# Decay rows of the state-space branch: from matmuls to DMA, with the order of the work around them rewritten

## The chip, the cores and the metric

The kernel runs on one core of a Trainium2 chip. The metric is the device time in microseconds (us) of one execution. Three executions of the kernel before took 2516.0, 2516.44 and 2516.64 us; the median is 2516.44 us.

## The reference, cut to what matters

Two blocks of two layers each work on 512 positions of 1024 features. The change touches the first block, once in each of its two layers:

```python
h = rmsnorm(x, attn_norm_g[layer])
proj = h @ w_in[layer]
gm_u, gm_v, ssm_z, ssm_xbc, ssm_dt, da_q, da_k, da_v, gates = split_cols(proj, IN_SIZES)
y_a = chunked_spatial_gating(gelu(gm_u), gelu(gm_v), ...)
y_b = mamba2_mixer(ssm_z, ssm_xbc, ssm_dt, ...)
...
merged = g[:, :, 0] * (y_a @ w_branch_a[layer]) + g[:, :, 1] * (y_b @ w_branch_b[layer]) + ...
```

Inside `mamba2_mixer` lies the scan over four chunks of 128 positions, for 16 heads of 64 features:

```python
a_cum = jnp.cumsum(dtc * a, axis=2)
decay = exp(where(causal, a_cum[t] - a_cum[s], -inf))
y_diag = einsum('bctsgh,bcsghp->bctghp', cb[..., None] * decay, xdt)
states = einsum('bcsgn,bcsgh,bcsghp->bcghpn', bc, decay_end, xdt)
y_off  = einsum('bctgn,bcghpn,bctgh->bctghp', cc, prev, exp(a_cum))
y = y_diag + y_off + d_skip * x
```

For each head the row `a_cum` over all 512 positions is wanted on all 128 partitions: `decay` has position t along the row and position s along the partitions, and `exp(a_cum)` scales the columns of `cc`.

## The kernel before, in words

**Matmuls.** Each product with a weight is made of three float32r matmuls over 512 columns (`mm3`, L571 to L573): high part by high part, low by high, high by low. Weights come in slabs. A slab of 8 tiles of 128x128 (512 KB) is 24 matmuls; a slab of `w_branch_a` has 4 tiles (256 KB, 12 matmuls).

**A slab's way.** SyncE (SP) issues its load (`load`, L545) once the slab four places earlier has been used, since `w_raw` has four places. ScalarE (ACT) makes the high part (`hi_ahead`, L561), VectorE (DVE) the low part (`lo_ahead`, L566), both three slabs ahead of TensorE (PE). All engines work through fixed programs, each in its own order, with semaphores between them; all DMAs that load weights are issued by SP on one queue.

**Order of PE in a layer of block 1:** the slabs `gv`, `xbc` (12), `z` (8), `gu` (4), `gate_a` (8), `a` (8), `qkv` (12) and on. A bank of the accumulator `pg` holds one result; ACT or DVE must empty it before the fourth next. The small matmuls of the branches use the four banks of `pm`, numbered by the schedule `PM`.

**Scan.** `ac_keep` holds `a_cum` as 16 rows (heads) by 512. DVE splits it into two float32r parts in `ac_parts` (L1499, L1500). `ac_rows(p)` multiplies them by a column of `head_row` that stands in 128 columns, once for each head of pair p: 16 heads, 16 matmuls of 512 columns a layer (L2244), each of which puts one row on all partitions of a `pm` bank. From that bank, for each head: DVE takes the minimum with the head's column into `seg` (L1535, `bounded`), ACT makes `c_dec`, the exponential of chunks 1 to 3 (L1019), and the exponentials of the four chunks of `seg` (L1021); POOL multiplies `c_dec` by C (L2074) and the odd head's `seg` by `cb` (L2077), DVE the even head's (L1574). `seg` and `c_dec` have four places, two pairs. `y_pair(p)` (L2269, L2272) is the 14 small matmuls of a pair; DVE adds its result to `yf` (L1570).

**Where these stand.** The states of chunks 0 to 2 (L2252) are made after `gate_a` slabs 2, 4 and 6, from products that POOL makes (L2067). `ac_rows(0)` follows the last of them. In the `a` slabs PE goes: `ac_rows(p)`, slab p, `y_pair(p-1)`; the last pair falls into `qkv`. DVE in the same loop: minimum of pair p, low part of a slab, `m_val` times the slab's result (L1566), the addition (L1570), the product of the even head.

Of the kernel before, what the change touches and what calls it, by code (L numbers as in the profile page):

```python
# [7 lines left out]
F32 = mybir.dt.float32  # L8
# [105 lines left out]
def program(nc, t, out, depth=DEPTH, depth2=DEPTH):  # L114
    with ExitStack() as ctx:
# [53 lines left out]
        head_row = sb("head_row", [P, SSM_H], F32R)  # L169
# [80 lines left out]
        wt_gm = conv_in[:, 0, 4:4 + SEQ].rearrange("p (g n) -> p g n", g=GM_G)  # L250
# [6 lines left out]
        xw = [conv_in[:, 2 + g, 4:4 + SSM_I // SSM_G] for g in range(SSM_G)]  # L257
# [8 lines left out]
        ac_parts = over("ac_parts", arena_at + 4 * 26624, [P, SEQ], F32R)  # L266
# [51 lines left out]
        for name, slabs, units in [("gv", 4, 4), ("dt", 0, 1), ("xbc", 12, 12), ("z", 8, 8), ("gu", 4, 4), ("gate_a", 8, 8), ("a", 8, 8), ("qkv", 12, 12),  # L318
                                   ("gate_b", 8, 8), ("b", 8, 8), ("gate_c", 8, 8), ("c", 8, 8), ("out", 8, 8), ("up", 44, 44), ("down", 24, 8)]:
            SL.take(name, slabs)  # L320
            UN.take(name, units)
        for name, n in [("sums1", 1), ("spread1", 1), ("dt_n", 1), ("xs_n0", 2), ("ac_last", 1), ("xs_n", 6), ("gm_wt", 1), ("b_n", 2), ("cb", 2), ("gm_mix", 4)]:
            PM.take(name, n)
# [3 lines left out]
        for p in range(PAIRS + 1):  # L327
            if p < PAIRS:
                PM.take(("ac_row", p), 2)
            if p >= 1:  # L330
                PM.take(("y", p - 1), 1)
# [157 lines left out]
        def gate_unit(i):  # L489
# [10 lines left out]
                "gm_vn": TT, "decay_in": 1, "decays": 1, "dt_ready": TT, "ac_split": 1, "gm_wt_ready": 1, "ya_ready": GM_G, "ya_hi_done": GM_G,  # L500
                "ya_split": GM_G, "ac_zeroed": 1, "cb_masked": SSM_G, "seg_bound": SSM_H, "seg_exp": SSM_H, "y_init": KD, "c_exp": SSM_H, "c_scaled": SSM_H, "decay_cb_even": PAIRS, "decay_cb_odd": PAIRS, "y_sq": KD, "y_sq_added": KD - 1, "xw_ready": SSM_G * (TT - 1), "y_gated": KD, "y_rms": 1, "y_inv": 1,
                "yb_ready": KD, "yb_hi_done": 8, "yb_split": 8, "qk_ssq": TT, "qk_rms": 1, "qk_ready": 1, "lam_dot": 1, "lam_exp": 1,
                "neg_max": 2 * DA_H * TT, "w_ready": DA_H * TT, "sub_summed": 1, "sub_rms": 1, "yt_ready": DA_H, "gates_b": 1, "gate_a_last": 1, "b_merged": KD, "gates_c": 1,
# [362 lines left out]
        def _(act):  # L866
# [24 lines left out]
            act.wait_ge(setup, 8)  # L891
# [22 lines left out]
            for l in range(depth):  # L914
# [81 lines left out]
                for g in range(GM_G):  # L996
                    bank = unit_filled(act, SL["gu"] + g, UN["gu"] + g)
                    nc.scalar.activation(ya[:, g, :], bank, ACT.Gelu_apprx_tanh).then_inc(bank_free[(UN["gu"] + g) % BANKS], 1)
# [1760 lines left out]
```

## Time and profile before

| | |
|---|---|
| median of three executions | 2516.44 us |
| span of the profiled execution | 2514.7 us |
| PE busy | 2505.0 us |
| DVE, ACT, POOL busy | 1605.5, 1186.3, 317.8 us |
| granted clock of TensorE | 1.00 in every stretch asked for between 100 and 300 us |

The profiled execution's own total is not given apart from its span; its span is 1.7 us below the median of the three. A busy share says how much of the span an engine worked; a chain of waits says who stopped whom. Matmuls overlap, so the distance between the starts of two matmuls is what one costs, not its duration.

### The profile page before, as it was taken

The numbers are of one execution on the slowest core, as the hardware profiler recorded it, in microseconds if no ns is written. First come the engines' busy times: TensorE is split into PE (matmuls) and PEld (weight loads), VectorE is DVE, ScalarE is ACT, GpSimd is POOL, SyncE is SP. The second block draws the span as 40 slices with busy tenths as digits, with TensorE's granted clock in tenths as the row PEclk, the third lists the DMA queues.
The fourth block names the chain that finished last, engine by engine and source line by source line (L and its number), as shares of the span: only waits on it lengthen the run. The fifth ranks groups of instructions, "written<-read, shape, count | busy, mean of one in ns | idle before, by whom it ended". The sixth has DMA issues, their size and how long they took to land.

```text
span 2514.7 us, 34027 instructions
## 1 busy us (share of the span) xinstructions
PE 2505.0 (100%) x12261; PEld 2048.5 (81%) x12261; DVE 1605.5 (64%) x2461; ACT 1186.3 (47%) x2185; POOL 317.8 (13%) x248
## 2 busy tenths in 40 slices
PE   9999999999999999999999999999999999999999
PEld 7887887888888887887877888888888777887777
DVE  6735767567777347538767567774355777647765
ACT  6534545544333235436354443333246555564563
POOL 1024201010111000225020101110020001210010
PEclk9999999999999999999999999999999999999999
DMA  6433342333333353452444333333324322332322
GB/s 143 95 83 66 87 92 75 65 112 93 100 92 98 97 112 88 88 80 71 92 81 69 96 92 100 92 99 96 99 79 108 86 62 62 91 93 76 84 59 76
DMA packets 400031, 221.94 MB, mean 88 GB/s; under 512 B 52736, under 2 KB 377376, under 8 KB 399648
## 3 DMA queue, kind: packets, MB, share of 16 engines
q1 hardware_dynamic: 399904, 220.26, 35.7%
q8 instruction: 79, 1.29, 0.2%
q14 instruction: 48, 0.39, 0.1%
HBM read 218.12 MB, written 2.10 MB: 88 GB/s over the span
## 4 chain that ended last, share of the span: by engine, by line
PE 96%; DVE 2%; ACT 1%; issue 1%; DMA 1%; SPq 0%; DVEq 0%
PE pg L571 29%; PE pg L572 28%; PE pg L573 28%; PE pm L671 3%; PE pm L2465 1%; PE pm L2349 1%; PE pm L2439 1%; PE pm L2314 1%; PE pm L2269 1%; DVE w_lo L566 1%; PE pm L2479 1%; PE pm L2506 1%; ACT w_hi L561 0%; PE pm L2272 0%; PE pm L2252 0%
## 5 line engine op out<-in xcount | busy, mean ns | idle before, releaser
L566 DVE TENSOR_TENSOR w_lo<-w_raw,w_hi 128x1024 fp32r<-128x1024 f32 (+3 forms) x440 | 538.8, 1226 | 516.3 <-ACT w_hi L561 514.4
L571 PE MATMUL pg<-h_hi,w_hi 128*128 128x512 f32 x1856 | 737.1, 397 | 0.3 <-ACT arena L1229 0.2
L573 PE MATMUL pg<-h_hi,w_lo 128*128 128x512 f32 x1856 | 723.3, 390 | 0.0
L572 PE MATMUL pg<-h_lo,w_hi 128*128 128x512 f32 x1856 | 723.1, 390 | 0.0
L561 ACT ACTIVATE w_hi<-w_raw 128x1024 fp32r<-128x1024 f32 (+3 forms) x440 | 434.1, 988 | 588.4 <-DMA w_raw<-in_w_in_dram 239.5
L571 PEld LDWEIGHTS pg<-h_hi,w_hi 128*128 128x128 f32 x1856 | 348.6, 188 | 77.6 <-issue 8.9
L573 PEld LDWEIGHTS pg<-h_hi,w_lo 128*128 128x128 f32 x1856 | 348.4, 188 | 73.4
L572 PEld LDWEIGHTS pg<-h_lo,w_hi 128*128 128x128 f32 x1856 | 348.9, 188 | 69.5 <-issue 1.4
L571 PE MATMUL pg<-w_hi,h_hi 128*128 128x512 f32 (+2 forms) x440 | 164.9, 375 | 0.0
L573 PE MATMUL pg<-w_hi,h_lo 128*128 128x512 f32 (+2 forms) x440 | 162.0, 368 | 0.0
L572 PE MATMUL pg<-w_lo,h_hi 128*128 128x512 f32 (+2 forms) x440 | 161.9, 368 | 0.0
L1743 DVE SCALAR_TENSOR_TENSOR arena<-conv_in,par,arena 128x512 f32<-128x512 f32 x176 | 131.9, 749 | 15.3 <-DVE arena L1743 11.0
L571 PE MATMUL pg<-f_hi,w_hi 128*128 128x512 f32 x352 | 136.9, 389 | 0.0
L572 PE MATMUL pg<-f_lo,w_hi 128*128 128x512 f32 x352 | 136.9, 389 | 0.0
L573 PE MATMUL pg<-f_hi,w_lo 128*128 128x512 f32 x352 | 136.9, 389 | 0.0
L1143 ACT ACTIVATE arena<-conv_in,par 128x512 f32<-128x512 f32 x88 | 71.9, 817 | 127.0 <-DVE conv_in L1737 127.0
L555 POOL TENSOR_TENSOR f_lo<-arena,f_hi x44 | 57.9, 1317 | 516.3 <-DVE f_hi L1751 516.3
L1737 DVE TENSOR_TENSOR conv_in<-pg,rinv 128x512 f32<-128x512 f32 x88 | 60.8, 691 | 80.7 <-PE pg L573 80.6
L571 PE MATMUL pg<-nb_parts,w_hi 128*128 128x512 f32 x256 | 101.9, 398 | 0.0
L573 PE MATMUL pg<-nb_parts,w_lo 128*128 128x512 f32 x256 | 99.7, 389 | 0.0
L571 PEld LDWEIGHTS pg<-w_hi,h_hi 128*128 128x128 f32 x440 | 82.8, 188 | 13.8 <-issue 1.9
L572 PEld LDWEIGHTS pg<-w_lo,h_hi 128*128 128x128 f32 x440 | 82.9, 188 | 12.9 <-issue 1.0
(417 smaller groups left out, 3753.2 us busy)
## 6 DMA issues: line engine op xcount, KB each, us to landing
w_raw<-in_w_in_dram SPq DMA_DIRECT2D x184, 512.0 KB, 4.7
w_raw<-in_ffn_w_up_dram SPq DMA_DIRECT2D x88, 512.0 KB, 3.7
w_raw<-in_w_out_dram SPq DMA_DIRECT2D x32, 512.0 KB, 3.6
w_raw<-in_ffn_w_down_dram SPq DMA_DIRECT2D x32, 512.0 KB, 3.6
w_raw<-in_w_branch_b_dram SPq DMA_DIRECT2D x16, 512.0 KB, 3.5
w_raw<-in_ffn_w_down_dram SPq DMA_DIRECT2D x16, 384.0 KB, 3.2
w_raw<-in_w_branch_a_dram SPq DMA_DIRECT2D x16, 256.0 KB, 2.9
w_raw<-in_w_branch_c_dram SPq DMA_DIRECT2D x16, 256.0 KB, 2.8
```

The source lines that it names most:

```text
L555: return nc.gpsimd.tensor_tensor(lo, value, hi.bitcast(F32), ALU.subtract)
L561: nc.scalar.activation(w_hi[:, s % HI, 0:n], w_raw[:, s % RAW, 0:n], ACT.Copy).then_inc(hi_done, 1)
L566: nc.vector.tensor_tensor(w_lo[:, s % RAW, 0:n], w_raw[:, s % RAW, 0:n], w_hi[:, s % HI, 0:n].bitcast(F32), ALU.subtract)\
L571: nc.tensor.matmul(dst, l_hi, r_hi, start=start, stop=False)
L572: nc.tensor.matmul(dst, l_hi, r_lo, start=False, stop=False)
L573: return nc.tensor.matmul(dst, l_lo, r_hi, start=False, stop=stop)
L671: done = nc.tensor.transpose(dst, src, ident[0:src.shape[0], 0:src.shape[0]])
L1143: nc.scalar.activation(facc[:, j, :], conv_in[:, j, 4:4 + SEQ], ACT.Identity, bias=fconv_b[:, bass.ds(i, 1)], scale=fconv_w[:, i, 2:3]).th ...
L1737: nc.vector.tensor_tensor(conv_in[:, j, 4:4 + SEQ], unit_filled(dve, SL["up"] + j, UN["up"] + j, 4, it), inv[:, :], ALU.mult)\
L1743: nc.vector.scalar_tensor_tensor(facc[:, j, :], conv_in[:, j, 4 - a:4 - a + SEQ], fconv_w[:, i, 2 - a:3 - a], facc[:, j, :], ALU.mult, ALU ...
L2269: done = nc.tensor.matmul(bank[rows, c * P:(c + 1) * P], xdt[:, c, h * 64:h * 64 + 64], seg[:, h % 4, c, :], start=True, stop=c == 0)
L2314: done = nc.tensor.matmul(bank[:, qi * P:(qi + 1) * P], wt(h, kt)[:, (qi - kt) * P:(qi - kt + 1) * P], qkv[:, kt, 1024 + h * P:1024 + (h + ...
```

## The change

- The `ac_rows` matmuls, `head_row`, `ac_parts` and the two DVE instructions and the memset that filled it are gone. SP stores `ac_keep` to a DRAM tensor and loads each head's row from it onto 128 partitions, straight into `seg` (256 KB a head). Pairs 0 and 1 are loaded among the `z` slabs; the rows of pair p from 2 on behind the load of slab p+2 of `gate_a` and `a`, after a wait for `y_pair(p-2)`.
- ACT now makes `c_dec` from `seg` before DVE takes the minimum in place in `seg`.
- The `gu` slabs and the whole gated branch `ya` come ahead of `z`; the states are made behind slabs 4, 5 and 6 of `z`; `y_pair(p)` stands behind slab p of `gate_a`, then come the eight `a` slabs.
- The sigmoids of `gate_a` are made in two pieces after the eighth slab; before, seven were made straight from the bank. The squares of `y` move into the `a` slabs, their sum to the third `qkv` slab (before: the fourth).

```diff
-        for p in range(PAIRS + 1):
-            if p < PAIRS:
-                PM.take(("ac_row", p), 2)
...
+        for p in range(PAIRS):
+            PM.take(("y", p), 1)
...
@@ SP
+                def ac_rows(p):
+                    if p < 2:
+                        sp.wait_ge(S("rows_stored"), past("rows_stored") + 16)
+                        sp.wait_ge(S("ya_ready"), past("ya_ready") + GM_G)
+                    else:
+                        sp.wait_ge(pm_ready, PM[("y", p - 2)] + 1)
+                    for h in (2 * p, 2 * p + 1):
+                        sp.dma_start(seg[:, h % 4].rearrange("p c n -> p (c n)"), ac_rows_dram[l, h:h + 1, :].broadcast_to([P, SEQ])).then_inc(S(f"row_landed{h % 4}"), 16)
...
+                for i in range(2 * KD):
...
+                    load(sp, s, 0, 0, raw_view(s, w.shape[1] // P if i >= KD else KD, P), w_cols(w, l, c))
+                    if 4 <= i < PAIRS + 2:
+                        ac_rows(i - 2)
@@ ACT
+                def carried_exps(p):
+                    for h in (2 * p, 2 * p + 1):
+                        row_ready(act, h)
+                        nc.scalar.activation(c_dec[h % 4], seg[:, h % 4, 1:TT, :].rearrange("p c n -> p (c n)"), ACT.Exp).then_inc(S("c_exp"), 1)
...
+                for i in range(KD):
+                    gates(m_val, SL["gate_a"], UN["gate_a"], i, 1, ACT.Copy)
+                    hi_ahead(SL["gate_a"] + i)
+                    if i + 2 < PAIRS:
+                        carried_exps(i + 2)
+                        chunk_exps(i + 2)
@@ DVE
+                for p in range(PAIRS):
+                    lo_ahead(SL["gate_a"] + p, 0, 0)
+                    u = PM[("y", p)]
+                    nc.vector.tensor_tensor(yf[:, p, :], yf[:, p, :], pm_filled(dve, u), ALU.add).then_inc(pm_free[u % 4], 1)
+                    if p + 1 < PAIRS:
+                        even_decays(p + 1)
+                    if p + 2 < PAIRS:
+                        bounded(p + 2)
@@ PE
                 for p in range(PAIRS):
-                    if p >= 1:
-                        ac_rows(p)
-                    if p == 0:
-                        pe.wait_ge(S("ya_split"), past("ya_split") + GM_G)
-                    slab_t(pe, SL["a"] + p, UN["a"] + p, 0, 0, ya_hi, h_parts(ya_lo), 4)
-                    if p >= 1:
-                        y_pair(p - 1)
+                    slab_t(pe, SL["gate_a"] + p, UN["gate_a"] + p, 0, 0, hh, hl, KD)
+                    y_pair(p)
```

On SP, the DMAs of the changed kernel from the `gate_a` slabs on. `w_raw<-in_w_in_dram 128x8x128` is the load of a `gate_a` slab, `arena<-ac_rows` a row spread into `seg`:

```order
L542 DMA w_raw<-in_w_in_dram 128x8x128 x5
L2671 DMA arena<-ac_rows 128x512 x2
L542 DMA w_raw<-in_w_in_dram 128x8x128
L2671 DMA arena<-ac_rows 128x512 x2
L542 DMA w_raw<-in_w_in_dram 128x8x128
L2671 DMA arena<-ac_rows 128x512 x2
L542 DMA w_raw<-in_w_in_dram 128x8x128
L2671 DMA arena<-ac_rows 128x512 x2
L542 DMA w_raw<-in_w_branch_a_dram 128x4x128
```

Before, the loads of weights followed one another here with nothing between them. Now the two rows of pairs 2, 3, 4 and 5 each stand right behind the load of `gate_a` slab 4, 5, 6 and 7.

On ACT, the loop over the `gate_a` slabs of the changed kernel: L1000 empties a slab's bank, L558 makes a high part, L1006 is `c_dec`, L1013 the exponentials of chunks.

```order
L1000 ACTIVATE arena<-pg 128x512
L558 ACTIVATE w_hi<-w_raw 128x1024
L1006 ACTIVATE conv_in<-arena 128x384 x2
L1013 ACTIVATE arena<-arena,rinv 128x128 x8
L1000 ACTIVATE arena<-pg 128x512
L558 ACTIVATE w_hi<-w_raw 128x1024
```

Before, these exponentials stood among the `a` slabs and read the rows from `pm`. Now each high part stands behind two heads' exponentials, which wait for the rows' DMAs.

On DVE, the loop of the changed kernel: L563 is a low part, L1571 the addition to `yf`, L1535 the product of the even head, L1529 the two minima of the pair after it. Behind it stands the same place in the kernel before:

```order
L563 TENSOR_TENSOR w_lo<-w_raw,w_hi 128x1024
L1571 TENSOR_TENSOR arena<-arena,pm 128x512
L1535 TENSOR_TENSOR arena<-arena 128x512
L1529 TENSOR_TENSOR arena<-arena,rinv 128x512 x2
L563 TENSOR_TENSOR w_lo<-w_raw,w_hi 128x1024
```

```order
L1535 TENSOR_TENSOR arena<-pm,rinv 128x512 x2
L566 TENSOR_TENSOR w_lo<-w_raw,w_hi 128x512
L1566 TENSOR_TENSOR arena<-arena,pg 128x512
L1570 TENSOR_TENSOR arena<-arena,pm 128x512
L1574 TENSOR_TENSOR arena<-arena 128x512
```

The minima (L1535 before, L1529 now) read SBUF and no longer the accumulator, and the product of a pair now stands behind a full low part and an addition that itself waits for the pair before.

## Rows read from the trace of the kernel before

**Rows 1.** The page: span, and busy time of each engine
```profile
span 2514.7 us, 34027 instructions
...
PE 2505.0 (100%) x12261; PEld 2048.5 (81%) x12261; DVE 1605.5 (64%) x2461; ACT 1186.3 (47%) x2185; POOL 317.8 (13%) x248
```

**Rows 2.** Waits of PE: line, waited for, total us, times, longest
```profile
PE pm L2130 <- DMA arena<-in_norm_g_dram: 3.4, 1, 3.4
```

**Rows 3.** Timeline of PE around one pair: start, us, engine, line, operation
```profile
244.01 0.39 PE L573 MATMUL pg<-nb_parts,w_lo 128*128 128x512 f32 x1
...
246.80 0.40 PE L572 MATMUL pg<-ya_lo,w_hi 128*128 128x512 f32 x1
```

**Rows 4.** Timeline of PE around the last pair, which has no rows behind it
```profile
274.02 0.39 PE L573 MATMUL pg<-w_hi,h_lo 128*128 128x512 f32 x1
...
276.35 0.39 PE L572 MATMUL pg<-w_lo,h_hi 128*128 128x512 f32 x1
```

**Rows 5.** Loads issued at 189.7, 195.1, 1102.0, 1107.4 and 462.3 us: KB, us to landing
```profile
w_raw<-in_w_in_dram SPq DMA_DIRECT2D x1, 512.0 KB, 9.1
...
w_raw<-in_w_in_dram SPq DMA_DIRECT2D x1, 512.0 KB, 12.3
...
w_raw<-in_w_in_dram SPq DMA_DIRECT2D x1, 512.0 KB, 8.1
...
w_raw<-in_w_in_dram SPq DMA_DIRECT2D x1, 512.0 KB, 14.2
...
w_raw<-in_w_in_dram SPq DMA_DIRECT2D x1, 512.0 KB, 11.5
```

**Rows 6.** First `a` slab's load behind `gate_a` slab 7: landing, issue, load landing; then seven alone
```profile
216.43 1.06 ACT L561 ACTIVATE w_hi<-w_raw 128x1024 fp32r<-128x1024 f32 x1 [2.73 <-DMA w_raw<-in_w_in_dram]
...
213.22 0.37 SPq L545 DMA_DIRECT2D w_raw<-in_w_branch_a_dram  x1
...
w_raw<-in_w_branch_a_dram SPq DMA_DIRECT2D x1, 256.0 KB, 3.9
...
w_raw<-in_w_branch_a_dram SPq DMA_DIRECT2D x7, 256.0 KB, 2.9
```

**Rows 7.** A 2 KB row spread on 128 partitions behind a slab's load: issues, landings
```profile
897.65 0.37 SPq L545 DMA_DIRECT2D w_raw<-in_ffn_w_down_dram  x1
898.06 0.58 SPq L2601 DMA_DIRECT2D arena<-in_gm_b_s_dram  x1
...
w_raw<-in_ffn_w_down_dram SPq DMA_DIRECT2D x1, 512.0 KB, 3.6
arena<-in_gm_b_s_dram SPq DMA_DIRECT2D x1, 256.0 KB, 3.8
```

**Rows 8.** Timeline of ACT: a bank emptied, one head's exponentials, a high part
```profile
220.30 0.60 ACT L1004 ACTIVATE arena<-pg 128x512 f32<-128x512 f32 x1 [2.81 <-PE pg L573]
...
262.64 0.49 ACT L1019 ACTIVATE conv_in<-pm 128x384 f32<-128x384 f32 x1 [0.93 <-DVE arena L1535]
263.02 1.27 ACT L1021 ACTIVATE arena<-arena,rinv 128x128 f32<-128x128 f32 x4
...
265.74 1.05 ACT L561 ACTIVATE w_hi<-w_raw 128x1024 fp32r<-128x1024 f32 x1
```

**Rows 9.** Timeline of DVE in the same pair
```profile
261.83 1.29 DVE L1535 TENSOR_TENSOR arena<-pm,rinv 128x512 f32<-128x512 f32 x2 [0.60 <-PE pm L2244]
263.04 1.22 DVE L566 TENSOR_TENSOR w_lo<-w_raw,w_hi 128x1024 fp32r<-128x1024 f32 x1
264.17 0.68 DVE L1566 TENSOR_TENSOR arena<-arena,pg 128x512 f32<-128x512 f32 x1
```

**Rows 10.** Timeline of DVE and of POOL: a product in SBUF beside POOL's products
```profile
249.61 1.47 DVE L1574 TENSOR_TENSOR arena<-arena 128x512 f32<-128x512 f32 x1
...
247.99 2.54 POOL L2074 TENSOR_TENSOR sq<-sq,arena 128x384 f32<-128x384 f32 x2 [0.59 <-ACT sq L1019]
```

**Rows 11.** Timeline of POOL: the two products ahead of a pair of states
```profile
214.86 2.05 POOL L2067 TENSOR_TENSOR conv_in<-arena,rinv 128x512 f32<-128x512 f32 x2 [10.60 <-PE pm L2252]
```

More of the change, by code:

```diff
@@ L1004, in gates @@
                         nc.scalar.activation(dst[:, i, :], unit_filled(act, s + i, u + i), func).then_inc(bank_free[(u + i) % BANKS], 1)
-                act.wait_ge(S("y_init"), past("y_init") + KD)
-                for i in range(KD - 1):
-                    gates(m_val, SL["gate_a"], UN["gate_a"], i, 1, ACT.Sigmoid)
-                    hi_ahead(SL["gate_a"] + i)
-                act.wait_ge(pm_ready, PM[("state", TT - 2)] + SSM_G)
-                for p in range(PAIRS):
-                    if p >= 2:
-                        act.wait_ge(pm_ready, PM[("y", p - 2)] + 1)
+                def carried_exps(p):
@@ new lines, in _ @@
+                hi_ahead(SL["z"] + 1)
+                for p in range(2):
+                    carried_exps(p)
+                hi_ahead(SL["z"] + 2)
+                for p in range(2):
+                    chunk_exps(p)
+                z_in(0)
+                hi_ahead(SL["z"] + 3)
+                for g in range(SSM_G):
+                    left_of("b_n", bn, g)
+                for g in range(SSM_G):
+                    left_of("cb", cb, g)
+                for j in range(4, 7):
+                    hi_ahead(SL["z"] + j)
@@ L1035, in _ @@
+                for a in range(2):
+                    half = m_val[:, 4 * a:4 * a + 4, :]
+                    nc.scalar.activation(half, half, ACT.Sigmoid).then_inc(S("gates_a"), 1)
+                for i in range(KD):
+                    hi_ahead(SL["a"] + i)
                     act.wait_ge(S("y_gated"), past("y_gated") + i + 1)
@@ L1037, in _ @@
                     nc.scalar.activation(sq[:, i % 2, :] if i else sq_sum[:, :], yf[:, i, :], ACT.Square).then_inc(S("y_sq"), 1)
[L1038 removed]
+                for c in range(3):
                     hi_ahead(SL["qkv"] + c)
@@ L1581, in _, with y_square @@
-                lo_ahead(SL["qkv"], 0, 0)
-                for i in range(1, KD):
+                def y_square(i):
                     dve.wait_ge(S("y_sq"), past("y_sq") + i + 1)
@@ L2230, in _ @@
-                pe.wait_ge(S("gm_wt_ready"), past("gm_wt_ready") + 1)
-                pe.wait_ge(S("gm_vn"), past("gm_vn") + TT)
-                for g in range(GM_G):
-                    bank = take_pm(pe, PM["gm_mix"] + g)
-                    for c in range(TT):
-                        done = nc.tensor.matmul(bank[:, c * P:(c + 1) * P], gv[:, c, g * P:(g + 1) * P], wt_gm[:, g, :], start=True, stop=True)
-                    done.then_inc(pm_ready, 1)
-                def ac_rows(p):
-                    for h in (2 * p, 2 * p + 1):
-                        bank, row = take_pm(pe, PM[("ac_row", p)] + h % 2), head_row[:, h:h + 1].broadcast_to([P, P])
-                        if h == 0:
-                            pe.wait_ge(S("ac_split"), past("ac_split") + 1)
-                        nc.tensor.matmul(bank, row, ac_parts[:, :], start=True, stop=True).then_inc(pm_ready, 1)
@@ new lines, in _ @@
+                for g in range(SSM_G):
+                    bank = take_pm(pe, PM["cb"] + g)
+                    for c in range(TT):
+                        cs = slice(c * P, (c + 1) * P)
+                        done = nc.tensor.matmul(bank[:, cs], xb[:, 8 + g, cs], xb[:, 10 + g, cs], start=True, stop=True)
+                    done.then_inc(pm_ready, 1)
+                for j in range(4):
+                    slab_n(pe, SL["z"] + 4, UN["z"] + 4, hh, hl, 512, 4, 2, j, features=True)
+                    if j < TT - 1:
+                        pe.wait_ge(S("xw_ready"), past("xw_ready") + SSM_G * (j + 1))
```

314 lines of the change are left out of this document (151 added, 163 removed).

## The prediction, as it stood before the changed kernel ran

> **What bounds the kernel now.** I read the page first. PE is busy 2505.0 of 2514.7 us [rows 1], so a matmul removed is gained and an engine that makes PE wait is lost. The waits of PE come second: the longest is 3.4 us at the start [rows 2]; in the stretch that the change touches PE waits for nobody. Everything there is fed ahead of time, and the question is whether it still is. So I read the spacing of PE around a pair of heads, then the landing times of the loads that the rows will queue behind, then ACT and DVE, step by step, along the chain that prepares a pair.
>
> **Removed: the spreading matmuls.** From the last matmul of one slab to the second of the next takes 2.79 us with a pair and two spreading matmuls between [rows 3] and 2.33 us with a pair alone [rows 4]. Two of them cost 0.46 us; eight pairs in two layers give 16 x 0.46 = 7.4 us. No bound is needed: rows show both cases, and the order leaves none of the 32.
>
> **Natural pace of the new loop.** Slabs of `gate_a` take 5.4 us: their loads are issued at the ends of slabs, at 189.7 and 195.1 us [rows 5]. That is 0.227 us for each of 24 matmuls. A pair alone costs 2.33 less two such steps, 1.88 us. One turn is 7.32 us. I count from the end of `gate_a` slab 0: y(0) runs from 0 to 1.9, slab 1 ends at 7.3, y(2) would start at 14.6, y(3) at 22.0.
>
> **Added: rows behind slow loads.** SP issues slab 4's load at 0, the rows of pair 2 after y(0), slab 5's load at 7.3, the rows of pair 3 after y(1) at 9.2. The loads of slabs 4 and 5 are the slow ones: 9.1 and 12.3 us to landing in layer 0, 8.1 and 14.2 in layer 1, and 11.5 for `gate_c` slab 5, whose queue was empty [rows 5]. In the kernel before nobody minded, as they are needed 16 us after issue. Do rows wait for them? The first `a` load was issued at 213.2 while `gate_a` slab 7 was on its way (landed 216.4), and took 3.9 us, so landed at 217.1, 0.7 after it; alone such a load takes 2.9 [rows 6]. That is a queue in order. A 2 KB row spread on 128 partitions, issued at 898.06 behind a load of 897.65, landed at 901.86 against 901.25, 0.6 later [rows 7]. So a pair's two rows land at D+0.6 and D+1.2, where D is when the slab ahead lands. D4 is 9.1 in layer 0 and 8.1 in layer 1. D5 in layer 0 lies between 7.3+11.5 = 18.8 and 7.3+12.3 = 19.6; I take 19.2. In layer 1 it is 7.3+14.2 = 21.5.
>
> **From rows to y.** ACT makes the even head's `c_dec`, 0.49 [rows 8]: D+1.1. DVE's minimum starts 0.81 before ACT goes on [rows 8, 9]: D+1.9. Two heads take ACT from 262.64 to 265.74 [rows 8]; less two `c_dec` of 0.38 that is 1.17 for each head's exponentials: D+4.2. Then ACT empties a bank (0.60) and makes slab 4's (or 5's) high part (1.05) [rows 8]: D+5.9. DVE's low part takes 1.13 from start to start, the addition 0.68 [rows 9], the even product 0.68 like it (same form): D+8.4. The product of a pair stands behind a low part that has nothing to do with it, since ACT made that slab's high part after the exponentials. The upper bound has contention: a product in SBUF took 1.47 beside POOL's products [rows 10], 0.8 more. The minimum read the accumulator before and now reads SBUF, just as POOL starts on `c_dec`: D+9.2. I take D+9.0, nearer the end whose row has the same neighbours. POOL's own odd product, if it takes 1.5 like that one, is done by D+6.
>
> The Trainium skill (SBUF — State Buffer, section on the two separate sides) says that DVE with two SBUF inputs and a GpSimd instruction that reads SBUF exclude each other for a whole instruction. By that the minimum could wait a full POOL product, up to 2.54/2 = 1.3 us, and the total would be some 2 us higher; by the row alone it is the 0.8 above. The trace has the slower product, without showing why.
>
> **Sum of stalls.** y(2) starts at 9.1+9.0 = 18.1 (layer 0) and 17.1 (layer 1) instead of 14.6: stalls of 3.5 and 2.5. y(3) starts at 19.2+9.0 = 28.2 and 21.5+9.0 = 30.5, where without any stall it were 22.0: by then 6.2 and 8.5 us are lost in all. From pair 4 on, the rows come with slack: slab 6, issued at 14.7 and as slow as slab 4, lands at 23.8, which lets y(4) start at 32.8, and the natural start by then is 28.2+7.3 = 35.5. What counts is the ring of DVE and ACT from one pair's minimum to the next: 0.81 + 2.34 + 0.60 + 1.05 + 1.13 + 0.68 + 0.68 = 7.3, with contention 8.1; I take 7.7 against 7.32, 0.4 for each of pairs 4 and 5. Later splits are of `a` slabs, half as long. That is 0.8 a layer. Stalls: 6.2 + 8.5 + 1.6 = 16.3 us. Nothing gives it back, as PE is the bound behind it.
>
> Sum: 2514.7 - 7.4 + 16.3 = 2523.6 us of span. The median of the runs stands 1.7 above the span, so I forecast **2525 us**.
>
> **What I cost at nothing.** The `gu` slabs and `ya` ahead of `z`: same matmuls, each slab split three ahead, 16 us of cover. If ACT's longer queue (Silu, Gelu with their tables) broke it, PE would wait at `z`. The states behind `z` slabs 4 to 6: the first needs POOL's mask and two products of 2.05 us [rows 11] after `cb`, within one slab of 5.4; about 2 us of cover. If POOL ran late, each state would cost up to the 2.05. Pairs 0 and 1: their rows are loaded among the `z` slabs, more than five slabs ahead. The sixteen rows and the store cost SP an issue of about 0.4 us each [rows 7], while SP is idle; SP waits for y(p-2), with the next load queued behind, and that load needs a later slab's end anyway. The `a` slabs: DVE has four instructions of 0.68 against 12 matmuls of 0.227 = 2.72 us, and starts with three slabs split; next late would be `qkv` slab 0. Fewer changes of PE between kinds of matmul, under 0.5 us, are left out.
>
> **Rivals.**
>
> *Rows are not held (faster).* If rows land about 3 us after issue as in a free queue, the mechanism is absent. The place is the landing of pair 2's and 3's rows; from y(p-2)'s end to y(p)'s natural start there are 12.8 us, and the chain from the even row's landing takes 8.4, so the case decides if that row lands within 4.4 us. Then only the 7.4 us count: 2516.4 - 7.4 = 2509 us. For it: loads of other weights land in 3.6 [rows 7]. Against it: the queue in order [rows 6]. The Trainium skill (DMA: Bandwidth & Descriptors, queues, rings and completion order) says descriptors are consumed in order on each DMA engine, but nothing orders the 16 engines; if rows slipped by on most of them, the landing would still need the last. Chance 0.17.
>
> *Half the stall (no change).* The slow landings of slab 5 came with loads 5.4 us apart, now 7.3. If slab 5 lands as slab 4 does, 8.6 after issue, D5 is 15.9 and pair 3 is on time once pair 2 is late. Left are 3.5 + 2.5 and the ring's 1.6: 2516.4 - 7.4 + 7.6 = 2517 us. Against it: 11.5 us with an empty queue [rows 5]. Chance 0.21.
>
> *A second stall (slower still).* Beside all of the forecast, `z` waits for states, 2.05 for each of three, or the ring takes 8.1 for five pairs (4 us a layer instead of 0.8): 2525 + 6 = 2531 us. Chance 0.08.
>
> **How the numbers follow.** The forecast has 0.54. Its own range: the chain at 8.4, D5 at 18.8 and 21.5, and the ring at 7.3 give stalls of 5.2+7.9 = 13.1, so 2522; the chain at 9.2, D5 at 19.6 and 21.5, and the ring at 8.1 give 6.8+8.7+3.2 = 18.7, so 2528. The range of 8 in 10 reaches from the faster case to between forecast and second stall: 2509 to 2531. A measurement here can tell 0.2%, 5.0 us, from no change. Slower by more: 0.54 + 0.08 = 0.62. Within: the half stall, 0.21. Faster: 0.17.
>
> **What would show it.** In the profile of the changed kernel: no spreading matmuls; PE idle ahead of y(2) and y(3) in each layer, about 3 and 3 us in layer 0 and 3 and 6 in layer 1, and released by DVE's product; rows of pair 2 landing 8 us after issue and those of pair 3 11 us, just behind slabs 4 and 5; ACT waiting there for the rows' DMA. I am wrong if PE's waits are found elsewhere (at `z`, at the states, in the `a` slabs), if rows land within 4.4 us, or if the span is under 2515.

## The result, and the profile after

The changed kernel takes 2547.8 us (median of 4 runs, 2546.95 to 2554.86) against 2516.26 us beside it: a ratio of 1.0132, 95% interval 1.012 to 1.0143. It is slower by 31.5 us. The forecast was 2525 us with a range of 2509 to 2531: the sign is right, the size is not. In a later session the same kernel took 2543.7 us (1.011, 1.0094 to 1.0125), so 4 us lie between sessions. The experiments below were run in three later sessions, and the changed kernel was run again in the last of them alone. Their totals are set against its 2543.7, and a difference of under some 4 us to it says little by itself; where a stretch of the profile shows the same, it is given. The profiled execution took 2547.74 us, with 1.7 us around its span, as before.

The page of the changed kernel, in the lines that answer to [rows 1], and its line on the rows' DMAs (count, size, median time to landing):

```profile
span 2546.0 us, 33830 instructions
...
PE 2505.5 (98%) x12229; PEld 2046.1 (80%) x12229; DVE 1619.5 (64%) x2454; ACT 1193.0 (47%) x2187; POOL 316.9 (12%) x246
...
arena<-ac_rows SPq DMA_DIRECT2D x32, 256.0 KB, 6.5
```

PE's 32 spreading matmuls are gone, yet it is busy for as long as before: 2505.5 against 2505.0 us. The span is longer than its busy time by 40.5 us, where that was 9.7. What PE waits for, over the whole span (answers to [rows 2], where one wait of 3.4 us led the list):

```profile
PE pm L2287 <- DVE arena L1535: 11.8, 3, 4.5
PE pg L568 <- DVE arena L1591: 6.1, 4, 1.8
PE pm L2272 <- POOL arena L2093: 4.7, 2, 2.4
PE pm L2287 <- issue: 4.4, 5, 1.6
PE pm L2152 <- DMA arena<-in_norm_g_dram: 3.7, 1, 3.7
PE pg L568 <- DVE w_lo L563: 1.2, 1, 1.2
PE pg L568 <- ACT arena L990: 1.2, 2, 0.7
```

L2287 is the first matmul of a pair of heads, L1535 the even head's product; L1591 is the product with `m_val` that frees a bank in the `a` slabs; L2272 is a state, L2093 the product it is made from. The first was forecast; the fourth ("issue", waits for which the profile names no releaser) only in part, as 3.0 of its 4.4 us stand ahead of y(5) in the two layers, where the prediction had 0.4 each. The others (bar the fifth, which is the start of the program) stand in places that the prediction had costed at nothing.

The same by stretch. From `z` slab 4 to y(0), from y(0) to the first `a` slab, from there to the end of the second `qkv` slab, in layer 0 and then in layer 1; columns: length, then busy time and instructions of PE, PEld, DVE, ACT, POOL, granted clock, DMA share, GB/s.

```profile
164.88:201.87 36.99, 34.61 (x133) 25.34 (x133) 15.13 (x16) 10.62 (x16) 11.25 (x10) 0.95 0.27 60
201.87:263.91 62.04, 55.08 (x393) 44.55 (x392) 32.29 (x34) 33.10 (x78) 23.52 (x18) 0.97 0.41 101
263.91:300.24 36.33, 33.39 (x147) 26.99 (x146) 23.14 (x35) 17.19 (x21) 0.00 (x0) 1.00 0.52 106
...
1092.47:1127.80 35.33, 32.96 (x132) 24.61 (x133) 14.47 (x16) 10.62 (x16) 11.25 (x10) 1.00 0.37 63
1127.80:1191.92 64.12, 54.80 (x394) 44.48 (x393) 32.25 (x34) 33.11 (x78) 23.58 (x18) 0.97 0.48 98
1191.92:1228.51 36.59, 33.38 (x147) 26.98 (x145) 23.28 (x35) 17.19 (x21) 0.00 (x0) 1.00 0.48 107
```

What these stretches take when nothing holds PE (their natural length below) is known from the last two experiments: 32.7, 53.2 and 33.15 us. Against that the changed kernel loses 4.3 + 2.6 = 6.9 us at the states, 8.8 + 10.9 = 19.8 at the pairs, 3.2 + 3.4 = 6.6 in the `a` slabs and the first `qkv` slabs. Ahead of them, against the same work in the kernel before, 1.9 us are lost in both layers together between the first `gu` slab and `z` slab 4 (at `cb` and at a bank that ACT's Silu frees late), 1.5 us at `gu` slab 0 of layer 0. Sum: 36.7, less 7.4 for the matmuls removed, is 29.3. Of the remaining 2.0 us of the 31.3 between the spans, 1.0 is a wait for DVE in the feed-forward part and 0.3 a longer first wait; the other 0.7 is not placed, and why the wait in the feed-forward part is there in some kernels and not in others was not tried.

**The pairs.** The chain of y(2) in layer 0, to be read beside [rows 5, 8 and 9]. First what the issues of `gate_a` slab 4's load and of the even row say: issue, and time to landing.

```profile
L542 SPq DMA_DIRECT2D w_raw<-in_w_in_dram x1: 368/368/368, 202.0 to 202.0; - x1
...
DMA to landing us min/median/max: 9.6/9.6/9.6
...
L2671 SPq DMA_DIRECT2D arena<-ac_rows x1: 339/339/339, 203.7 to 203.7; - x1
...
DMA to landing us min/median/max: 8.6/8.6/8.6
```

The timeline behind them (start, us, engine, line, operation, idle before and for whom):

```profile
213.85 1.46 POOL L2069 TENSOR_TENSOR conv_in<-conv_in,arena 128x384 f32<-128x384 f32 x1
214.36 1.50 DVE L1529 TENSOR_TENSOR arena<-arena,rinv 128x512 f32<-128x512 f32 x1
...
214.78 2.39 ACT L1013 ACTIVATE arena<-arena,rinv 128x128 f32<-128x128 f32 x7
...
217.25 1.27 POOL L2075 TENSOR_TENSOR arena<-arena 128x512 f32<-128x512 f32 x1 [1.94 <-ACT arena L1013]
217.55 1.04 ACT L558 ACTIVATE w_hi<-w_raw 128x1024 fp32r<-128x1024 f32 x1
218.63 1.23 DVE L563 TENSOR_TENSOR w_lo<-w_raw,w_hi 128x1024 fp32r<-128x1024 f32 x1 [2.77 <-ACT w_hi L558]
219.77 0.68 DVE L1571 TENSOR_TENSOR arena<-arena,pm 128x512 f32<-128x512 f32 x1
220.37 0.68 DVE L1535 TENSOR_TENSOR arena<-arena 128x512 f32<-128x512 f32 x1
...
221.16 0.88 PE L2287 MATMUL pm<-arena 128*64 128x128 f32 x8 [4.50 <-DVE arena L1535]
```

Slab 4 lands at 211.6, the row 0.7 later, and y(2) starts 9.6 us after the slab: exponentials, high part, low part, addition, product, in the forecast's order. The chain is the forecast's, 0.6 us longer; a minimum takes 1.5 us beside POOL's products (the view starts at the second minimum of the pair; the first, from 212.90 on, took 1.5 as well).

**TensorE's clock.** Right behind the wait of 4.5 us (same columns as above, from 217 us on):

```profile
217.00:221.00 4.00, 0.00 (x0) 0.00 (x0) 2.37 (x3) 1.60 (x3) 1.27 (x1) 1.00 0.38 107
221.00:223.00 2.00, 1.84 (x20) 1.88 (x22) 0.68 (x2) 1.04 (x2) 0.65 (x1) 0.61 1.03 344
223.00:225.00 2.00, 2.00 (x14) 1.54 (x11) 2.00 (x2) 1.07 (x4) 1.75 (x2) 0.53 0.22 65
```

The granted clock falls to half, the 1.2 GHz level, for 3.4 us (221.4 to 224.8), and y(2) takes 2.94 us instead of 1.68; with the slab behind it the dip makes PE busy for 2.3 us more. In layer 1 it is 1.4, and behind the first state of layer 0 another 1.8. That is 5.5 of the 7.9 us between the busy time seen and the one that 7.4 us of removed matmuls should have left.

Busy time is not yet lost time. The dips behind y(2) add nothing to the span, for the next pair is not released by PE:

```profile
229.82 0.91 DVE L1535 TENSOR_TENSOR arena<-arena 128x512 f32<-128x512 f32 x1
```

y(3) of layer 0 starts at 230.84, 0.1 us behind the end of this product, the last step of the chain from slab 5's landing (221.1). At full clock PE would have stood there 2.3 us longer. In layer 1 PE even waits 2.8 us at y(3), after the dip. This is read from the chain and was not tried. At the first state nothing of the kind follows, and there the dip counts: in the second profile of this kernel, with a wait of 2.0 us and no dip, the same stretch took 34.95 us instead of 36.99.

**The states.** In layer 0, PE at state 0 (L2272), and ahead of it ACT (Silu with its table, high part, four copies of `bn` and `cb`; `bn` is the states' other factor) and POOL (two masks, two products):

```profile
162.85 1.28 ACT L990 ACT_TABLE_LOAD   x1
164.14 2.07 ACT L990 ACTIVATE arena<-pg 128x512 f32<-128x512 f32 x4
166.06 1.08 ACT L558 ACTIVATE w_hi<-w_raw 128x1024 fp32r<-128x1024 f32 x1
167.01 2.09 ACT L995 ACTIVATE arena<-pm 128x512 f32<-128x512 f32 x4
...
168.68 1.22 POOL L2082 TENSOR_SCALAR_AFFINE_SELECT arena<-arena 128x512 f32<-128x512 f32 x2 [5.35 <-ACT arena L995]
...
169.87 3.02 POOL L2093 TENSOR_TENSOR arena<-arena,rinv 128x512 f32<-128x512 f32 x2
172.95 3.12 PE L2272 MATMUL pm<-arena 128*128 128x512 f32 x4 [2.38 <-POOL arena L2093]
```

POOL idles 5.35 us for masks that the state does not need, then makes the products that it does.

**The `a` slabs.** ACT, DVE and PE where the first `qkv` slab wants the bank of `a` slab 6:

```profile
286.27 1.04 ACT L558 ACTIVATE w_hi<-w_raw 128x1024 fp32r<-128x1024 f32 x1
...
287.35 1.23 DVE L563 TENSOR_TENSOR w_lo<-w_raw,w_hi 128x1024 fp32r<-128x1024 f32 x1 [0.45 <-ACT w_hi L558]
288.49 0.68 DVE L1589 TENSOR_TENSOR arena<-arena 128x512 f32<-128x512 f32 x1
289.09 0.68 DVE L1591 TENSOR_TENSOR arena<-arena,pg 128x512 f32<-128x512 f32 x1
...
289.82 0.50 PE L568 MATMUL pg<-w_hi,h_hi 128*128 128x512 f32 x1 [1.12 <-DVE arena L1591]
```

DVE's product stands behind the low part of a `qkv` slab; that waits for ACT's high part, that for ACT's square, and that for DVE's gating behind the low part before: a ring of 3.5 us a turn (287.35 less 283.87, where the low part before it starts), while the 12 matmuls of an `a` slab take 2.7.

### The profile page after: what moved, and what is told of

Read it like the earlier page. It is cut to its first block, busy times and chain, and to the rows that moved or that the text cites. A ratio compares the mean times of both kernels' runs of the same rounds, so it can differ in the third digit from the quotient of the medians.

```text
span 2546.0 us, 33830 instructions
## 1 busy us (share of the span) xinstructions
PE 2505.5 (98%) x12229; PEld 2046.1 (80%) x12229; DVE 1619.5 (64%) x2454; ACT 1193.0 (47%) x2187; POOL 316.9 (12%) x246
## 3 DMA queue, kind: packets, MB, share of 16 engines
q1 hardware_dynamic: 404576, 228.71, 36.2%
## 4 chain that ended last, share of the span: by engine, by line
PE 91%; DVE 3%; DMA 3%; ACT 2%; issue 2%; POOL 0%; SPq 0%; DVEq 0%; POOLq 0%; ACTq 0%
PE pg L568 27%; PE pg L570 27%; PE pg L569 27%; PE pm L672 3%; DMA w_raw<-in_w_in_dram 2%; PE pm L2480 1%; ACT w_hi L558 1%; DMA arena<-ac_rows 1%; DVE w_lo L563 1%; PE pm L2364 1%; PE pm L2454 1%; PE pm L2329 1%; PE pm L2287 1%; DVE arena L1529 1%; PE pm L2494 1%
## 5 line engine op out<-in xcount | busy, mean ns | idle before, releaser
L563 DVE TENSOR_TENSOR w_lo<-w_raw,w_hi 128x1024 fp32r<-128x1024 f32 (+3 forms) x440 | 542.3, 1233 | 513.1 <-ACT w_hi L558 511.8
L558 ACT ACTIVATE w_hi<-w_raw 128x1024 fp32r<-128x1024 f32 (+3 forms) x440 | 434.2, 988 | 601.2 <-DMA w_raw<-in_w_in_dram 260.5
```

The costliest lines, as they stand in the source:

```text
L558: nc.scalar.activation(w_hi[:, s % HI, 0:n], w_raw[:, s % RAW, 0:n], ACT.Copy).then_inc(hi_done, 1)
L563: nc.vector.tensor_tensor(w_lo[:, s % RAW, 0:n], w_raw[:, s % RAW, 0:n], w_hi[:, s % HI, 0:n].bitcast(F32), ALU.subtract)\
```

## The experiments

Each is an edit of the changed kernel. Times are medians; the ratio is to the kernel before on the same chip.

**Rows not loaded.**

```diff
                     load(sp, s, 0, 0, raw_view(...), w_cols(w, l, c))
-                    if 4 <= i < PAIRS + 2:
-                        ac_rows(i - 2)
...
+                    if p >= 2:
+                        act.wait_ge(pm_ready, PM[("y", p - 2)] + 1)
                     for h in (2 * p, 2 * p + 1):
                         row_ready(act, h)
```

> This kernel leaves out the row loads of pairs 2 to 7: those pairs work on what their buffers hold from earlier pairs, and ACT waits for y(p-2) in the load's place. All other work is as in the changed kernel. Theory Q (rows wait in SP's queue behind the slow loads of gate_a slabs 4, 5 and 7): the stretch from y(0) to the end of y(7) loses about 8.8 us in layer 0 and 10.9 us in layer 1 against its natural pace, all of it goes, so 2547.8 - 19.7 = 2528 us (2525 to 2531), and PE's waits ahead of the pairs vanish. Theory R (the ring of DVE and ACT, one turn longer than PE's 7.36 us, sets the pace whatever the rows do): waits of 0.4 to 0.8 us remain ahead of five or six pairs in each layer, so 2534 to 2538 us. Both: the waits at the states (2.4 us each layer) and in the a slabs (about 3 us each layer) stay.

2531.8 us, ratio 1.0065 (1.0048 to 1.0082), just above theory Q's range and below theory R's. The pairs' stretch falls from 62.0 and 64.1 to 54.6 and 57.4 us: 14.1 us of the 19.8. Of the rest, two waits of 0.6 us in layer 0 are of theory R's kind; a single wait of 2.7 us ahead of y(3) in layer 1 (4.2 us with the dip of the clock behind it) is of neither, and the next kernel shows what it is. The stretch of the `a` slabs took 37.9 and 37.2 us here. In the kernels that do not touch it, it lies between 36.2 and 38.3, and the clock makes most of the difference: where the granted clock was at half for 3.4 us in it, as here in layer 0, it took 37.9 to 38.3, elsewhere 36.2 to 36.8, but for the 37.2 here in layer 1.

**Rows ahead of the load.**

```diff
+                    if 4 <= i < PAIRS + 2:
+                        ac_rows(i - 2)
                     load(sp, s, 0, 0, raw_view(...), w_cols(w, l, c))
-                    if 4 <= i < PAIRS + 2:
-                        ac_rows(i - 2)
```

> SP issues the rows of pair i-2 ahead of the load of gate_a slab i (i from 4) instead of behind it. Theory Q: the rows of pair 2 find slab 3's load just landed and take 3.2 us, y(2) is on time; those of pair 3 come behind slab 4's load, now issued 1.5 us later, and land in time for y(3) within 0.5 us; those of pair 4 come behind slab 5's load and make y(4) some 2 us late in layer 0 and 4 us in layer 1. Of 19.7 us some 6 stay: 2534 us (2530 to 2538). Rival (the rows themselves are slow, 128 copies of 2 KB beside weight loads, or the DVE and ACT ring sets the pace): 2543 to 2548 us.

2542.5 us, 1.0103 (1.0086 to 1.012): next to the rival's range (2543 to 2548), far from theory Q's. The pairs' stretch is 61.1 and 62.9 us. But the rows of pairs 2 and 3 did land early, those of pair 3 in 4.5 us at 213.1. The timeline of this kernel ahead of y(3) in layer 0:

```profile
222.77 1.06 ACT L558 ACTIVATE w_hi<-w_raw 128x1024 fp32r<-128x1024 f32 x1 [3.13 <-DMA w_raw<-in_w_in_dram]
...
223.86 1.23 DVE L563 TENSOR_TENSOR w_lo<-w_raw,w_hi 128x1024 fp32r<-128x1024 f32 x1 [6.59 <-ACT w_hi L558]
...
225.00 0.68 DVE L1571 TENSOR_TENSOR arena<-arena,pm 128x512 f32<-128x512 f32 x1
225.60 0.89 DVE L1535 TENSOR_TENSOR arena<-arena 128x512 f32<-128x512 f32 x1
...
226.59 1.12 PE L2287 MATMUL pm<-arena 128*64 128x128 f32 x8 [3.79 <-issue]
```

DVE sits idle for 6.6 us with pair 3's exponentials long done: it waits to split slab 5, whose load has just landed, and the product stands behind that split. The slow load is a second gate, by way of ACT's and DVE's order, with no row in it.

**Rows on ACT's own queue.**

```diff
+                        for h in (2 * p, 2 * p + 1):
+                            act.dma_start(seg[:, h % 4]..., ac_rows_dram[l, h:h + 1, :].broadcast_to([P, SEQ]))...
```

SP's own calls of `ac_rows` from pair 2 on go.

> The rows of pairs 2 to 7 are issued by ACT, on ACT's own DMA queue, after y(p-2); SP's queue holds weight loads alone. Theory Q (order within one queue holds the rows): they land 3 to 4.5 us after issue even beside the loads of slabs 4 and 5, the chain of about 9 us then ends within the 12.8 us that there are, and 2547.8 less 18 gives 2530 us (2526 to 2534). Rival D (the 16 DMA engines behind the queues are held by the slow loads, whichever queue a packet comes from): the rows land 7 to 11 us after issue as now and the time stays within 4 us of 2547.8.

2543.5 us, 1.0107 (1.009 to 1.0124), the time of the changed kernel. The even row of pair 2, on ACT's queue, and slab 4's load, on SP's:

```profile
L1007 ACTq DMA_DIRECT2D arena<-ac_rows x1: 352/352/352, 199.1 to 199.1; - x1
...
DMA to landing us min/median/max: 8.5/8.5/8.5
...
L542 SPq DMA_DIRECT2D w_raw<-in_w_in_dram x1: 368/368/368, 197.4 to 197.4; - x1
...
DMA to landing us min/median/max: 9.5/9.5/9.5
```

The row still lands 0.7 us behind the slab. So a place behind the load in SP's queue is not needed to hold it, and theory D forecast the landing of pair 2. For pair 3 the test is weaker, as ACT issued those rows only after its exponentials (at 211.3), but they too landed behind their slab: the even row at 217.0 after 5.7 us, slab 5 at 216.4. What holds the rows, if not their place in a queue, no run here tells apart. The Trainium skill (DMA: Bandwidth & Descriptors, section on issuing engines not being separate DMA queues) says that DMAs of all issuing engines run on the same 16 DMA engines, and that spreading them saves issue time only. The trace agrees: 8.5 us against 8.6.

**Other columns for slabs 4 and 5.**

```diff
-                    w, c = (w_in, C_GATE + P * i) if i < KD else ...
+                    w, c = (w_in, C_GATE + P * (i - 4 if i in (4, 5) else i)) if i < KD else ...
```

> gate_a slabs 4 and 5 load the columns of slabs 0 and 1, so the gate's values of those two slabs are of other columns; sizes, order and work are the same. Theory A (the slow landing belongs to the columns, that is to the addresses): slabs 4 and 5 land in 5.5 to 7.5 us after issue as slabs 0 to 2 do, rows of pairs 2 and 3 land 4 us and 5 to 7 us earlier, and the time falls by 10 to 14 us to 2534 to 2538. Theory B (the landing belongs to the place in the program, to what else the DMA engines and HBM do then): slabs 4 and 5 keep 9.6 and 11.8 us in layer 0, 9.8 and 13.7 in layer 1, and the time stays at 2547.8.

2542.0 us, 1.01 (1.0083 to 1.0117). In layer 0 slab 4 lands in 6.0 us and pair 2's rows in 5.0, as theory A has it (7.4 and 6.3 in layer 1); but slab 5 took 9.0 and 9.9 and slab 6, still on its own columns, 10.0 and 11.5. PE's waits of 2 us and more came at y(3) in layer 0, and at y(2), y(3) and y(4) in layer 1 (2.2, 2.5, 3.2). Theory A for the landing of slab 4, a miss for slab 5 and for the time. A cleaner test follows below.

**The even product ahead of the low part.**

```diff
                 for p in range(PAIRS):
+                    if p + 1 < PAIRS:
+                        even_decays(p + 1)
                     lo_ahead(SL["gate_a"] + p, 0, 0)
...
-                    if p + 1 < PAIRS:
-                        even_decays(p + 1)
```

> On DVE the even product of pair p+1 is issued ahead of the low part of gate_a slab p+3 and of the addition of y(p), instead of behind them; nothing else differs from the changed kernel, rows stay behind the slow loads. Theory G (two gates: the rows that land behind slabs 4 and 5, and DVE's product, which stands behind the low part of that same late slab): the chain from row to y shrinks from 9.1 to 9.6 us to some 5.5 to 6, so y(2) waits about 1.2 us and y(3) about 2 to 4 us in each layer, the wait ahead of y(5) goes, and PE's clock is not lowered: 2547.8 less 11 is 2537 us (2534 to 2540). Theory L (only the landing of the rows and ACT's exponentials decide, the product's place is hidden): 2545 to 2548 us.

2536.3 us, 1.008 (1.0063 to 1.0096), inside theory G's range. The pairs' stretch is 57.5 and 62.0 us. The clock fell once in it all the same, behind the wait of 4.0 us in layer 1. PE now waits for POOL, whose odd product is last:

```profile
PE pm L2287 <- POOL arena L2075: 10.5, 4, 4.0
```

**Rows first and product first.** Both edits together.

> Both: SP issues the rows of pair i-2 ahead of the load of slab i, and DVE makes the even product ahead of the low part. Theory G: with rows first alone y(3) still waited 3.8 us in layer 0 and 5.7 us in layer 1 although its rows had landed 13 us before, because the product stood behind the low part of slab 5, whose load landed 3.9 us before y(3). With that gate gone as well only pair 4, whose rows come behind slab 5's load, can be 0 to 2 us late: 2547.8 less 17 is 2531 us (2528 to 2534), with less than 1.5 us of waits at any pair. Rival (ACT, whose exponentials of pair 3 stand behind the high part of slab 4 and those of pair 4 behind that of slab 5, holds the pairs by itself): y(4) waits 3 us or more and the time is 2537 to 2542 us.

2533.2 us, 1.0065 (1.0048 to 1.0081). The stretch is 55.5 and 58.7 us: 2.3 and 5.5 over the natural pace, at pair 4 alone, released by POOL's odd product (3.9 us the longest). By the order, its rows and the high part that ACT makes ahead of its exponentials both wait for slab 5. The total fits G, the single wait fits the rival; rows alone gave 1 us, the product alone 7, both 10.5: two gates in a row, of which one edit opens only one. The pairs' stretches of both layers together say the same without the difference between sessions: 126.2 us in the changed kernel (124.9 in its second profile), 124.0 with the rows first, 119.5 with the product first, 114.3 with both.

**POOL's products ahead of its masks.**

```diff
-                for g in range(SSM_G):
-                    pm_left(pool, PM["cb"] + g)
-                    nc.gpsimd.affine_select(out=cb[:, g], ...)
...
                         nc.gpsimd.tensor_tensor(by64(xw[g]), ...).then_inc(S("xw_ready"), 1)
+                    if c == 0:
+                        for g in range(SSM_G):
+                            pm_left(pool, PM["cb"] + g)
+                            nc.gpsimd.affine_select(out=cb[:, g], ...)
```

> POOL makes the two xw products of state 0 ahead of the two masks of cb instead of behind them (it sat idle for 5 us before the masks, which wait for ACT's copies of cb). If the order on POOL is what makes z slab 5 late, PE's waits for POOL ahead of the first state (2.4 us in each layer) vanish, and with them the stretch at the lower clock behind the one in layer 0 (1.8 us): 2547.8 less 6 is 2542 us (2540 to 2544). Rival: the state then waits for ACT's copy of bn or its banks instead, over 1.5 us in each layer, and the time stays above 2544.5 us. Nothing changes in gate_a and in the a slabs.

2537.3 us, 1.0095 (1.0078 to 1.0111), below the expected 2540 to 2544, which were counted from 2547.8. The waits at the states are gone and that stretch is 32.7 us in both layers: 6.9 less than in the first profile. Against 2543.7 the whole gained 6.4.

**Gating and product ahead of the low part in the `a` slabs.**

```diff
-                    lo_ahead(SL["a"] + i, 0, 0)
                     pm_left(dve, PM[("y", i)])
                     nc.vector.tensor_tensor(yf[:, i, :], yf[:, i, :], zf(i), ALU.mult)...
                     nc.vector.tensor_tensor(m_val[:, i, :], ...)...
+                    lo_ahead(SL["a"] + i, 0, 0)
```

> In the a slabs DVE makes the gating of yf and the product of m_val (which frees a PSUM bank) ahead of the low part of slab a+i+3 instead of behind it. If the banks come free late because the products stand behind low parts that wait for the high parts of the first qkv slabs, whose loads landed late, PE's waits for L1591 (1.1 and 1.8 us in layer 0, 1.4 and 1.8 us in layer 1) vanish: 2547.8 less 6 is 2542 us (2540 to 2544). Rival (the two sigmoids of 1.9 us and ACT's squares set the pace there): waits of 1 us and more remain and the time stays above 2545 us.

2536.6 us, 1.0084 (1.0067 to 1.0101), below its range too. The four waits for L1591 are gone; the stretch is 33.2 and 33.1 us, 6.6 less than in the first profile. The two sigmoids of 1.9 us did not matter.

**The changed kernel again.**

> The changed kernel itself, once more, beside the others. xw first and the product ahead of the low part each gave 10 to 11 us where the waits in their own stretch add up to 6 to 7, so either they help elsewhere or the changed kernel's time in those jobs is lower than the 2547.8 measured first. If it is the spread of this kernel between jobs, this run gives 2542 to 2545 us; if the edits help elsewhere, it gives 2547 to 2549 us.

2543.7 us. So this kernel differs by 4 us between sessions, and the two single edits before gave 6.4 and 7.1 us, not 10 and 11. Its profile also shows that the losses move. The stretch of the `a` slabs in layer 0 and a part of it:

```profile
259.50:297.75 38.25, 35.01 (x146) 28.11 (x145) 23.85 (x35) 17.19 (x21) 0.00 (x0) 0.96 0.48 100
289.50:292.90 3.40, 3.40 (x9) 2.62 (x8) 2.07 (x3) 0.65 (x1) 0.00 (x0) 0.50 0.00 0
```

Here the clock fell among the `a` slabs, in both layers (38.3 and 38.0 us), and not at the states (35.0 and 34.8). The states lost 4.4 us in this execution, the pairs 18.5 and the `a` slabs 9.9, where the first profile has 6.9, 19.8 and 6.6.

**Permuted columns.**

```diff
-                    w, c = (w_in, C_GATE + P * i) if i < KD else ...
+                    w, c = (w_in, C_GATE + P * ((i + 4) % KD)) if i < KD else ...
...
-                    gates(m_val, SL["gate_a"], UN["gate_a"], i, 1, ACT.Copy)
+                    nc.scalar.activation(m_val[:, (i + 4) % KD, :], unit_filled(...), ACT.Copy)...
```

> The eight gate_a slabs take their columns in the order 4, 5, 6, 7, 0, 1, 2, 3, with the same slots, banks, rows and waits; the gate's values go to the tiles of their columns. Theory A (slow landing belongs to the columns): slabs at places 4 to 7 land in 5 to 8 us, those at places 0 and 1 in 9 to 14 us, issued among the z slabs where they are needed 21 us later; y(2) waits under 1.5 us, y(3) 1 to 3 us, and the stretch from y(0) to the a slabs falls from 62.0 and 64.1 us to 55 to 58 in both layers: 12 us less than the changed kernel beside it. Theory B (it belongs to the place): the stretch keeps 61 to 64 us. A risk of A: the split of the slow slabs now stands in DVE's and ACT's order ahead of the states' work, and PE waits at the states grow by 1 to 3 us.

2537.0 us, 1.0082 (1.0068 to 1.0096): 6.7 us less, where 12 were expected. The eight columns in us to landing, changed kernel against this one, in layers 0 / 1:

```
column    0        1        2        3        4        5        6        7
changed  5.7/5.6  7.3/8.0  5.2/5.7  6.9/9.2  9.6/9.8 11.8/13.7 8.8/10.1 7.5/9.9
permuted 6.0/7.1  8.8/9.8  7.0/7.7  6.4/7.8  8.3/8.0 10.8/13.1 7.8/10.2 6.7/8.4
```

Column 5 is slowest in both places, by far: the landing belongs mostly to the columns (theory A). The rest, up to some 2 us either way, goes with the place; what in it was not tried, and the rows' own DMAs are only a guess. Why these addresses are slow stays open. The stretch fell only to 58.8 and 59.5 us because 8.8 and 9.8 us at place 5 are still too much: the loop leaves 14.7 us from that load's issue to y(3), the row and the chain need 9.6 behind the landing, and y(3) waits 3.0 us in either layer.

**All four edits.**

> Four edits at once: rows ahead of the load, even product ahead of the low part, xw ahead of the masks, gating and product ahead of the low part in the a slabs. The waits named so far add up: the stretches of the states and of the a slabs run at their natural 32.7 and 33.1 us, the stretch of the pairs keeps 2.3 and 5.5 us over its natural 53.2 (POOL's odd product at pair 4). 2544 less 7 for the states, 7 for the a slabs and 14 for the pairs is 2516 to 2519 us, about the time of the kernel before. Rival (one stretch's wait moves into the next): 2522 us and more.

2519.5 us, 1.0013 (1.0003 to 1.0022), half a us above the range expected. The gains add: 6.4 + 7.1 + 10.5 is 24.0, and 2543.7 less 2519.5 is 24.2. That close a fit is luck, as the single edits were run in another session; the firmer evidence is that the stretches run as expected: 32.7 us at the states in both layers, 54.6 and 58.8 at the pairs, 33.6 and 33.2 in the `a` slabs. The waits left there are pair 4's (1.3 and 3.9 us) and one of 0.5 us for L1590.

**All four edits and the permuted columns.**

> The four edits and the permuted columns. If all waits between y(0) and the a slabs come from the slow loads at places 4 and 5, that stretch runs at 53.2 to 54.5 us in both layers, and the total is that of the kernel before less the 7.4 us of spreading matmuls, plus 1 to 3 us that remain at the gu slabs, at cb and z: 2509 to 2513 us, faster than both kernels. Rival (the slow loads among the z slabs hold states or y(0)): 2514 to 2520 us.

2512.5 us, ratio 0.9985 (0.9976 to 0.9994), within the expected range: 3.8 us faster than the kernel before. From y(0) to the `a` slabs in layer 0 and 1, then `a` and the first `qkv` slabs in layer 0, in the columns used above:

```profile
195.82:249.02 53.20, 53.20 (x394) 43.04 (x393) 32.24 (x33) 33.88 (x78) 22.89 (x18) 1.00 0.44 117
1106.64:1159.84 53.20, 53.20 (x394) 43.06 (x393) 31.55 (x33) 33.78 (x78) 23.18 (x18) 1.00 0.49 118
249.02:282.17 33.15, 33.13 (x147) 27.06 (x145) 23.54 (x35) 17.07 (x21) 0.00 (x0) 1.00 0.55 117
```

PE never waits there, with all the rows' DMAs in place, and its granted clock is 1.00. DVE and ACT are busy for 32 and 34 of 53 us: they were late by order, not by load. The slow loads among the `z` slabs cost 0.7 us in layer 1.

## Why the prediction was wrong in size

- **Removed matmuls, 7.4 us: right.** A turn of the new loop takes 7.36 us (7.32 forecast). The kernel with all edits has 3.6 us of it left in the span. PE is idle there for 12.3 us, 2.6 more than in the kernel before, and busy for 2498.8, which is 6.2 less and not 7.4; the last 1.2 us are not placed.
- **Landing behind slow loads: right in its place and size, its cause not borne out.** Slab 4 landed in 9.6 and 9.8 us (9.1 and 8.1 taken), slab 5 in 11.8 and 13.7, the rows 0.6 to 0.7 and 1.2 to 1.3 behind. By y(3) 6.9 and 8.9 us were lost, where the forecast had 6.2 and 8.5. But the reason given was a queue in order, and on another queue the row took 8.5 us too.
- **The chain of 9.0 us: 9.6, past its upper bound of 9.2.** The bound charged one minimum with 0.8 us more [rows 9, 10], and the first did cost that. Both minima of the pair took 1.5 us beside POOL's products, and the second held ACT's exponentials by 0.3 more; the even row and `c_dec` took 0.2 to 0.3 longer than costed. The Trainium skill (SBUF — State Buffer, section on the two separate sides) has a DVE instruction with two SBUF inputs and a GpSimd instruction that reads SBUF exclude each other; twice 0.8 us more fits that, and does not prove it.
- **"From pair 4 on, the rows come with slack": failed.** The ring was charged with 0.8 us a layer. Pair 5's rows landed behind slab 7, issued at 230.2 and slow as well (7.5 us): y(5) waited 1.5 us, y(4) 0.3 to 0.4, in each layer. From y(3) on 4.0 us were lost in both layers together instead of 1.6. The pairs lost 19.8 us, not 16.3: 1.1 more by y(3), 2.4 behind it. The clock's dips behind y(2), which the sum did not have either, are not a further term, as y(3) hung on DVE's product.
- **"What I cost at nothing": the step that failed most, 18.9 us with 2.0 that lie outside its places.** *States:* "about 2 us of cover" was counted from `cb` on PE to the products on POOL, but between them stood ACT's table load, four Silus, a high part and four copies, 6.2 us. The bound of 2.05 for each state was in the text and its chance at 0.08. It was 6.9 us for both layers, 1.8 of them the clock's. *`a` slabs:* instructions were counted (four of 0.68 against 2.72), not what each waits for; the ring with ACT took 3.5 us a turn once `qkv` slabs were being split. 6.6 us. *`gu` and `z`:* 3.4 us, with `gu` slab 0 in 10.1 us another slow load.
- **The rivals.** Rows held in no way (2509), and half the stall (2517), are out: the rows landed 8.6 us and more after issue, and PE's waits for pairs 2 and 3 were there in both layers. The second stall had the right kind and a price of 6 us where 22 were added.

In sum: 2523.6 + 3.5 + 18.9 = 2546.0 us, the span of the changed kernel in its first profile. The sum closes by its making, since the last 2.0 are what was left over.

## What to carry to other kernels

Where an engine works in order, ask of each instruction that is waited for what else stands ahead of it and what that waits for: a product behind the split of a slab waits for that slab's load, though it has nothing to do with it. Cover must be counted through every engine of the chain, and an engine that is half idle can still be late. Put the work that the bound engine waits for first, and fetch-ahead work, which has slabs of slack, behind it: three such swaps, the rows ahead of the load, and slow columns loaded where nothing urgent is behind them, turned +27 us into -4.

## What the runs showed of the hardware that was not expected

- A row's DMA on ACT's queue took 8.5 us beside a load issued 1.7 us earlier on SP's, as on one queue (8.6).
- A slab of `w_in` in 512-byte pieces landed in 5.2 to 13.7 us in the changed kernel, mostly by its columns: column 5 took 11.8 and 13.7 us at place 5 and 10.8 and 13.1 at place 1. Loads of the same size from other weights take 3.6 [rows 7]. Why is open.
- After idle stretches of 2.4 us (states, layer 0) and 4.5 us (pairs) the granted clock of TensorE was at half for 3.4 us, but not after 2.4 us at the states in layer 1 and not after 2.8 us at y(3) in layer 1. In the `a` slabs waits of 1.4 and 1.8 us in layer 0 were enough in the second profile of the same kernel, and waits of 1.4 and 1.8 us in layer 1 were not in the first. So two executions of one kernel differ by where the clock falls. What decides was not tried.
- A DVE minimum of 512 columns with both inputs in SBUF took 1.5 us beside POOL's products, a product of the same size alone 0.68.
